# Routing stage of a two-layer MoE backbone rebuilt, and Hyena filter spectra summed on TensorE

## The chip, the cores and the metric

One NeuronCore of one Trainium2 chip runs the whole program. The metric is device time in microseconds of one execution, as a median of several runs. Engines are named as the profile names them: PE (TensorE), DVE (VectorE), ACT (ScalarE), POOL (GpSimd), SP (SyncE, which here only issues DMAs). All arithmetic is in float32.

## The reference, cut to what matters

The step runs two trunk layers on 128 context tokens and 256 latent tokens (384 together): an attention layer, a Hyena layer, and after each a hierarchical mixture of experts (top group of 4, then top 2 of the 8 experts in it; 32 experts of width 256).

```python
def hier_moe(h, ...):                       # once per layer
    g_w, g_i = top_k(softmax(t @ w_grp + b_grp), 1)
    e_logits = (t @ w_rt + b_rt).reshape(n, 4, 8)[arange(n), g_i[:, 0]]
    e_w, e_i = top_k(softmax(e_logits), 2)
    weights = e_w / sum(e_w) * g_w
    ...                                     # gates: one weight per token and expert
    hg, hu = t @ w_gate[e], t @ w_up[e]
    y = sum over e of (silu(hg) * hu * gates[:, e]) @ w_down[e]

def fft_longconv(u, kf, skip):              # twice in the Hyena layer, FFT length 2L
    y = irfft(rfft(u, 2 * L) * kf, 2 * L)[:L]
    return y + u * skip
```

`kf` is the spectrum of a filter made by a small network of the positions. The context group has L = 128 and the latent group L = 256.

## The kernel before

The engines run five separate programs and meet at semaphores; `sig(name).by` counts up after an instruction and `sig(name).at` waits. PSUM is eight banks of 128 x 512; `open_` takes the next bank (or a named one) and waits until its last reader has finished. A float32 matmul shows as several records.

**The MoE layer** (`moe(l)` on each engine, run for l = 0 and 1) has two parts. The *routing stage* starts when the last residual tile is normed. PE turns the normed tokens (`transposes`) and multiplies by the router (`logits`, three tiles of 128 tokens), then keeps itself busy with five dummy products (`keep_busy(5)`) while DVE picks group and experts. PE counts tokens per expert (`count`) and ranks them (`rank`, nine products, each of the three token tiles ending in one that waits for the count). DVE turns ranks into slots, and PE inverts that list (`pref`, `inv`): 768 slots in six tiles, ordered by expert. POOL then gathers the token rows of the six slot tiles out of DRAM by six indirect DMAs (L1842). PE sends four rows of tokens to all partitions (`rows`, from `diag`, twelve DVE products at L1288), then turns the six gathered tiles (L757, eight transposes a tile), and ACT and DVE evict half a tile each (`xs_a`, `xs_d`) into `XS`. After three more dummy products come the experts.

The *expert loop* goes through 32 experts in order, one *step* per 32 slots of an expert, and at least one. In a step POOL copies 32 slots of `XS` into `xcur` (L1859), PE multiplies by the gate and up weights (`hidden`), by the down weights of the step before (`down_product`), adds the step before's rows to the token sums (`first_half`, `second_half`) and regroups (`summed`), with ACT, DVE and POOL between. The first step has no step before; its sums are opened with zeros (`zeroed`). Weights stand in a ring of four expert slots of 3 MB. SP issues the loads of the first four experts as soon as the residual is done (`load_experts`), and each later one when ACT has freed its slot (`gu_free`, `down_free`).

**The Hyena layer** convolves two halves of 512 channels, twice (b = 0 to 3). For each b PE makes the filter's taps (`taps`, three products), their norms and six *spectra* K (`filter_spectra`): real and imaginary parts for the context group and for the even and odd positions of the latent group, of which two also get the skip term by a product of one row (`trow`). ACT copies four spectra out of PSUM, two of them into `KE`; DVE then adds and subtracts the other two (`combined`, four operations a b) to get the latent filter `KF`. PE makes the signal's spectra (`signal_spectra`, ten products), DVE multiplies (`product`), PE goes back (`inverse`), DVE gates (`gated`). The six signal spectra U and the six K share banks 0 to 5. While DVE multiplies for b, PE makes the spectra of b + 1, with four dummy products (`warm`) among them.

Of the kernel before, what the change touches and what calls it, by code (L numbers as in the profile page):

```python
# [25 lines left out]
P = 128  # L26
# [148 lines left out]
def build(nc, a, stage=99):  # L175
    ctx = ExitStack()
    with ctx:
# [245 lines left out]
        KE = v(WORK + 9232, 2, 512)  # L423
# [46 lines left out]
        def _(pe):  # L470
# [230 lines left out]
            def moe(l):  # L701
# [10 lines left out]
                logits(0)  # L712
                logits(1)
                transposes(u, (2,))
# [28 lines left out]
                for r in range(4):  # L743
                    i = l * 4 + r
                    o = open_(pe, "rows", i, [("posr" if r < 2 else "wr", l * 2 + r % 2)])
                    sig("diag").at(pe, i)
                    for t in range(T):
                        last = mm(o[:, t * P:(t + 1) * P], ones, diag[:, r, t, :])
                    close(last, "rows", i)
                for i in range(ST):  # L750
                    pe.wait_ge(rows_gathered[i], 16 * (l + 1))
                    for j in range(2):
                        n = (l * ST + i) * 2 + j
                        o = open_(pe, "xs", n, [("xs_a" if j == 0 else "xs_d", l * ST + i)])
                        for k in range(4):
                            c = (4 * j + k) * P
                            last = pe.transpose(o[:, k * P:(k + 1) * P], slot_rows[:, i, c:c + P], ident)  # L757
                        close(last, "xs", n)
                keep_busy(3)
                first = turn[0] + turn[0] % 2  # L760
                acc = [(("acc", l * 6 + i), [("xffn", l * 3 + (1 if i < 4 else 2))], (first + 2 + i) % 8) for i in range(6)]
# [94 lines left out]
            def hyena():  # L856
# [44 lines left out]
                def filter_spectra(b, j0, j1):  # L901
                    sig("filt").at(pe, b * 6 + 5)
                    for j in range(j0, j1):
# [4 lines left out]
                        if j >= 4:  # L908
                            sig("skip").at(pe, b * 2 + j - 4)
                            last = mm(o, ones[0:1, :], trow[j - 4][0:1, :], False, True)  # L910
# [1214 lines left out]
```

## Time and profile before

| | us |
|---|---|
| median of 3 runs (lowest, highest) | 1252.37 (1250.38, 1256.89) |
| the profiled execution | 1246.98 |
| its span, first to last instruction | 1245.2 |
| PE busy (share of the span) | 1131.2 (91%) |
| DVE busy | 563.9 (45%) |
| ACT busy | 266.5 (21%) |
| POOL busy | 176.0 (14%) |
| mean granted TensorE clock | 0.956 |

The profiled execution lies 5.4 us below the median. All times in rows are microseconds from the span's start. The granted clock is a share of 2.4 GHz: 1.00 is 2.4 GHz and 0.50 is 1.2 GHz, and a stretch between these was partly at either.

### The profile page before, as it was taken

The numbers are of one execution on the slowest core, as the hardware profiler recorded it, in microseconds if no ns is written. First come the engines' busy times: TensorE is split into PE (matmuls) and PEld (weight loads), VectorE is DVE, ScalarE is ACT, GpSimd is POOL, SyncE is SP. The second block draws the span as 40 slices with busy tenths as digits, with TensorE's granted clock in tenths as the row PEclk, the third lists the DMA queues.
The fourth block names the chain that finished last, engine by engine and source line by source line (L and its number), as shares of the span: only waits on it lengthen the run. The fifth ranks groups of instructions, "written<-read, shape, count | busy, mean of one in ns | idle before, by whom it ended". The sixth has DMA issues, their size and how long they took to land.

```text
span 1245.2 us, 26266 instructions
## 1 busy us (share of the span) xinstructions
PE 1131.2 (91%) x9219; PEld 647.4 (52%) x9220; DVE 563.9 (45%) x1222; ACT 266.5 (21%) x648; POOL 176.0 (14%) x261
## 2 busy tenths in 40 slices
PE   6899979989878899999699999999998888999995
PEld 4654656644654455555555654444546544555553
DVE  1031265544443344444633334787555344444445
ACT  2111244440121112212322113221011211221211
POOL 0153120000021111121100001111001111122220
PEclk9999999999788899999899998999996898999998
DMA  9856899740859899999831221000039599987893
GB/s 361 298 191 226 278 331 324 244 147 3 357 226 419 350 415 375 422 422 410 304 113 68 92 78 68 0 1 1 29 106 423 205 421 421 419 348 293 333 421 149
DMA packets 82735, 314.21 MB, mean 252 GB/s; under 512 B 11160, under 2 KB 12097, under 8 KB 57321
## 3 DMA queue, kind: packets, MB, share of 16 engines
q1 hardware_dynamic: 77658, 300.56, 62.1%
q0 software_dynamic: 1952, 6.90, 1.4%
q10 hardware_dynamic: 3056, 5.77, 1.2%
q8 instruction: 51, 0.84, 0.3%
q14 instruction: 18, 0.15, 0.0%
HBM read 307.82 MB, written 5.39 MB: 252 GB/s over the span
## 4 chain that ended last, share of the span: by engine, by line
PE 81%; DVE 5%; DMA 4%; issue 4%; ACT 2%; SPq 2%; POOL 1%; POOLq 0%; ACTq 0%; DVEq 0%
PE banks L472 78%; DMA arena<-in_ada_b 3%; DVE arena L1038 3%; DMA arena<-token_rows,arena 1%; PE banks L669 1%; SPq L1938 1%; PE banks L757 1%; ACT arena L1649 1%; SPq L1936 1%; ACT arena L1659 1%; DVE arena L1188 1%; POOL arena L1842 0%; PE banks L880 0%; PE banks L615 0%; PE banks L523 0%
## 5 line engine op out<-in xcount | busy, mean ns | idle before, releaser
L472 PE MATMUL banks<-arena 32*128 32x256 f32 (+10 forms) x8792 | 1076.0, 414 | 73.1 <-issue 34.2
L472 PEld LDWEIGHTS banks<-arena 128*32 128x32 f32 (+3 forms) x8792 | 595.0, 152 | 530.3 <-issue 402.0
L1038 DVE TENSOR_TENSOR arena<-banks,arena 128x64 f32<-128x64 f32 (+3 forms) x282 | 113.1, 413 | 65.6 <-PE banks L472 59.9
L1038 DVE TENSOR_TENSOR arena<-arena 128x384 f32<-128x384 f32 (+13 forms) x229 | 132.4, 584 | 4.4
L1307 DVE SCALAR_TENSOR_TENSOR arena<-arena 128x768 f32<-128x768 f32 x81 | 84.8, 1047 | 107.5 <-issue 105.2
L1693 ACT ACTIVATE arena<-banks 128x512 f32<-128x512 f32 x79 | 47.2, 597 | 230.6 <-PE banks L472 230.6
L1850 POOL TENSOR_TENSOR arena<-arena 128x256 f32<-128x256 f32 x81 | 59.1, 730 | 229.9 <-PE banks L472 229.9
L1317 DVE TENSOR_SCALAR arena<-arena 128x64 f32<-128x64 f32 x79 | 15.4, 195 | 163.9 <-ACT arena L1697 163.9
L1859 POOL COPY arena<-arena 128x256 f32 x79 | 34.7, 439 | 188.2 <-PE banks L472 148.6
L1829 POOL TENSOR_SCALAR arena<-arena 128x8 f32<-128x8 f32 (+2 forms) x28 | 6.8, 244 | 316.4 <-ACT arena L1540 229.0
L1407 DVE TENSOR_SCALAR arena<-arena 128x385 f32<-128x385 f32 x24 | 11.6, 481 | 82.4 <-ACT arena L1754 82.4
L1319 DVE RECIPROCAL arena<-arena 128x64 f32<-128x64 f32 x79 | 43.7, 554 | 2.7
L1697 ACT ACTIVATE arena<-banks 128x64 f32<-128x64 f32 x79 | 17.7, 224 | 127.3 <-PE banks L472 127.3
L1050 DVE COPY arena<-banks 128x128 f32<-128x128 f32 x24 | 7.0, 291 | 75.2 <-PE banks L472 75.2
L1689 ACT ACTIVATE arena<-banks 128x256 f32<-128x256 f32 x79 | 30.4, 384 | 42.4 <-PE banks L472 42.4
L1540 ACT ACTIVATE arena<-arena 128x1024 f32<-128x1024 f32 x12 | 12.7, 1056 | 113.1 <-DVE arena L1038 111.2
L1871 POOL TENSOR_TENSOR arena<-arena 128x512 f32<-128x512 f32 x4 | 5.1, 1263 | 208.9 <-DVE arena L1038 208.9
L1649 ACT ACTIVATE arena<-banks,arena 128x384 f32<-128x384 f32 (+1 forms) x48 | 24.0, 506 | 39.4 <-DVE arena L1189 31.4
L1830 POOL TENSOR_TENSOR arena<-arena 128x8 f32<-128x8 f32 (+2 forms) x28 | 30.5, 1091 | 2.4 <-POOL arena L1829 0.2
L1753 ACT ACTIVATE arena<-banks,arena 128x128 f32<-128x128 f32 x24 | 8.9, 369 | 100.3 <-PE banks L472 100.3
L1117 DVE TENSOR_REDUCE arena<-arena 128x8 f32<-128x512 f32 (+1 forms) x13 | 9.7, 745 | 43.3 <-ACT arena L1589 23.2
L669 PE MATMUL banks<-arena 128*128 128x128 f32 x112 | 16.8, 279 | 11.1 <-ACT arena L1659 11.0
(152 smaller groups left out, 456.6 us busy)
## 6 DMA issues: line engine op xcount, KB each, us to landing
arena<-in_moe_w_gate SPq DMA_DIRECT2D x64, 1024.0 KB, 8.0
arena<-in_moe_w_up SPq DMA_DIRECT2D x64, 1024.0 KB, 10.3
arena<-in_moe_w_down SPq DMA_DIRECT2D x64, 1024.0 KB, 10.6
arena<-in_ada_w SPq DMA_DIRECT2D x24, 2048.0 KB
arena<-in_hy_w_in SPq DMA_DIRECT2D x6, 2048.0 KB
arena<-in_attn_w_in SPq DMA_DIRECT2D x3, 2048.0 KB
arena<-mod_rows SPq DMA_DIRECT2D x8, 512.0 KB, 9.1
arena<-in_attn_w_out SPq DMA_DIRECT2D x2, 2048.0 KB
```

Source lines behind the costliest of these rows:

```text
L472: return pe.matmul(out, lhsT, rhs, start=start, stop=stop, skip_group_check=True)
L669: last = pe.transpose(o[:, b * P:(b + 1) * P], PB[i % 2][:, r, b, :], ident)
L1038: return dve.tensor_tensor(o, p, q, op)
L1307: return dve.scalar_tensor_tensor(parts, posr, first_row[:, bass.ds(c, 1)], wr, ALU.is_equal, ALU.mult)
L1319: dve.reciprocal(e2, e1).then_inc(s_["moe_dve"], 1)
L1649: ins = act.activation(PB[i % 2][:, r, 0:n, :].rearrange("p b k -> p (b k)"), ps[:, 2 * (i % 2) + r, 0:n * P], ACT.Exp, bias=negmax[:, c:c ...
L1689: act.activation(ysb, py, ACT.Copy).then_inc(s_["moe_y"], 1)
L1693: act.activation(gsb.rearrange("p i q f -> p (i q f)"), pg, ACT.Copy).then_inc(s_["moe_g"], 1)
L1697: act.activation(ex, pt[:, 0:2 * M].rearrange("p (f m) -> p f m", f=2), ACT.Exp, scale=-1.0).then_inc(s_["moe_e"], 1)
L1830: sig(name).by(pool.tensor_tensor(dst, dst, half_[:, 0:n], ALU.pow), i)
L1850: return pool.tensor_tensor(*two, bc(ones, 2), ALU.mult)
L1859: pool.tensor_copy(xcur, XS[:, :, bass.ds(first, M)]).then_inc(s_["moe_x"], 1)
```

## The change

Routing stage:

- The order of PE's first products is tiles 0, 1, logits 0, tile 2, logits 1, logits 2 (before: logits 1 ahead of tile 2).
- `rank` is four products in place of nine, one of them behind the count. `keep_busy(2)` behind it is gone.
- The two rows of gate weights are sent to all partitions ahead of `pref` and `inv`, the two rows of positions behind, as before. `diag` is four broadcast products of 128 x 384 in place of twelve of 128 x 128; two of them stand ahead of the slot arithmetic on DVE. `lanes` is one operation in place of six.
- The accumulators have fixed banks 2 to 7 and the six slot tiles are turned through the same banks. PE turns slot tiles 0 to 2, runs `hidden` of the first step, and then turns tiles 3 to 5. `keep_busy(3)` is gone.
- POOL reads the first expert's step count and copies its 32 slots as soon as slot tile 0 is evicted, ahead of its loop; the first expert's further steps, if any, and then experts 1 to 31 follow.
- SP issues the load of the fourth expert only when PE has turned slot tile 3.

Hyena stage: the combined spectra are summed in PSUM (cosine or sine of the even positions, plus or minus that of the odd ones), so `KE`, `combined` and the DVE operations in it are gone, and ACT copies six spectra per b. `warm` is gone. Three of the six spectra get the skip row.

```diff
                 transposes(u, (0, 1))
                 logits(0)
+                transposes(u, (2,))
                 logits(1)
-                transposes(u, (2,))
...
-                for t in (2, 1, 0):
-                    for s in range(t + 1):
-                        mm(o[:, t * NE:(t + 1) * NE], upper if s == t else ones, both[:, s, :], s == 0, False)
-                    sig("count").at(pe, l)
-                    last = mm(o[:, t * NE:(t + 1) * NE], cc[0:NE, 0:P], upE, False, True)
-                close(last, "rank", l)
-                keep_busy(2)
+                mm(o[:, 0:3 * NE], upper, both.rearrange("p t e -> p (t e)"), True, False)
+                mm(o[:, NE:3 * NE], ones, both[:, 0:2, :].rearrange("p t e -> p (t e)"), False, False)
+                mm(o[:, 2 * NE:3 * NE], ones, both[:, 0, :], False, False)
+                sig("count").at(pe, l)
+                close(mm(o[:, 0:3 * NE].rearrange("p (t e) -> p t e", t=T), cc[0:NE, 0:P], bc(upE, T, 1), False, True), "rank", l)
...
+                turn_rows(0)
+                turn_rows(1)
                 sig("steps").at(pe, l)
...
-                for i in range(ST):
-                    pe.wait_ge(rows_gathered[i], 16 * (l + 1))
-                    for j in range(2):
...
-                keep_busy(3)
+                turn_rows(2)
+                turn_rows(3)
...
+                turn_slots((0, 1, 2))
+                pe.wait_ge(gu_loaded[0], 32 + l * 32 * (NE // 4))
+                hidden(0, 0)
+                turn_slots((3, 4, 5))
...
-                        src, t, m = ((PM, 0, s128), (PM, 1, se), (PM, 2, so), (PF, 2, co), (PF, 0, c128), (PF, 1, ce))[j]
+                spectra = ((PM, ((s128, 0),), None), (PM, ((se, 1), (so, 2)), None), (PM, ((se, 1), (nso, 2)), None),
+                           (PF, ((ce, 1), (co, 2)), 1), (PF, ((ce, 1), (nco, 2)), 1), (PF, ((c128, 0),), 0))
...
-                filter_spectra(0, 2, 4)
+                filter_spectra(0, 2, 3)
                 taps(1, 0)
-                filter_spectra(0, 4, 6)
+                filter_spectra(0, 3, 6)
...
-                        warm(b, 4)
-                        filter_spectra(b + 1, 2, 4)
+                        filter_spectra(b + 1, 2, 3)
...
-                for c in range(6):
-                    ins = dve.tensor_scalar(lanes[:, c, :], lane, lane_of[:, c:c + 1], None, ALU.is_equal)
-                sig("lo").by(ins, l)
+                sig("lo").by(tt(lanes, bc(lane, 6, 1), bc(lane_of, P, 2), ALU.is_equal), l)
...
-                        tt(KF[:, 2 + im, :], e, o, ALU.add)
-                        sig("K_dve").by(tt(KF[:, 4 + im, :], e, o, ALU.subtract), b * 2 + j)
...
+                sig("pref").at(pool, l)
+                n, b = steps_of(pool, 0)
...
+                sig("xs_a").at(pool, l * ST)
+                sig("xs_d").at(pool, l * ST)
+                pool.wait_ge(s_["moe_pg"], 1)
+                pool.tensor_copy(xcur, XS[:, :, 0:M]).then_inc(s_["moe_x"], 1)
...
                 for s in range(4):
+                    if s == 3:
+                        sig("psum_xs").at(sp, (l * ST + 3) * 2 + 1)
                     one(s, s, None)
```

## Rows read from the trace of the kernel before

**Rows 1.** Page, chain that ended last: share of the span by engine.

```profile
PE 81%; DVE 5%; DMA 4%; issue 4%; ACT 2%; SPq 2%; POOL 1%; POOLq 0%; ACTq 0%; DVEq 0%
```

**Rows 2.** Windows: length, busy per engine (instructions), PEclk, DMA share, GB/s.

```profile
314.40:364.50 50.10, 39.58 (x192) 32.09 (x192) 23.73 (x79) 9.01 (x18) 7.89 (x13) 0.73 0.86 346
364.50:605.00 240.50, 221.23 (x2456) 118.74 (x2457) 103.51 (x229) 45.96 (x115) 43.18 (x76) 0.97 0.95 387
...
819.23:850.96 31.73, 31.73 (x77) 12.88 (x76) 25.25 (x37) 6.72 (x8) 3.99 (x4) 1.00 0.00 1
...
928.80:980.48 51.68, 42.19 (x198) 34.65 (x198) 23.71 (x79) 10.43 (x19) 7.93 (x13) 0.70 0.83 336
```

**Rows 3.** Timeline, first routing stage, end: start, duration, engine, line, [idle before <- releaser].

```profile
343.59 1.12 POOL L1842 DMA_INDIRECT arena<-token_rows,arena  x1 [23.70 <-DVE arena L1280]
...
350.04 0.93 POOL L1842 DMA_INDIRECT arena<-token_rows,arena  x1 [0.30 <-issue]
...
354.26 6.29 PE L757 MATMUL banks<-arena 128*128 128x128 f32 x40 [1.12 <-DMA arena<-token_rows,arena]
...
364.04 0.40 POOL L1859 COPY arena<-arena 128x256 f32 x1 [13.06 <-issue]
...
364.49 4.70 PE L472 MATMUL banks<-arena 128*32 128x512 f32 x48 [1.84 <-POOL arena L1859]
...
367.42 1.37 PEld L472 LDWEIGHTS banks<-arena 128*128 128x128 f32 x16 [0.33 <-ACT arena L1693]
```

**Rows 4.** Windows of 4 us around the gathers of the first routing stage.

```profile
340.00:344.00 4.00, 2.45 (x12) 2.35 (x12) 1.74 (x9) 0.00 (x0) 0.41 (x1) 0.50 1.01 422
...
356.00:360.00 4.00, 3.95 (x31) 3.71 (x30) 2.63 (x4) 1.81 (x4) 0.00 (x0) 0.84 0.37 149
...
368.00:372.00 4.00, 3.68 (x45) 1.72 (x44) 1.66 (x5) 0.72 (x2) 0.81 (x2) 1.00 0.22 45
```

**Rows 5.** DMA issues: median us from issue to landing, gathers (512 KB each) and outputs.

```profile
arena<-token_rows,arena POOLq DMA_INDIRECT x6, 9.2
...
out_y_sample<-arena ACTq DMA_DIRECT2D x2, 512.0 KB, 2.6
```

**Rows 6.** Timeline, DVE: slot arithmetic, and an operation of 128 x 384.

```profile
336.09 0.35 DVE L1038 TENSOR_TENSOR arena<-arena,banks 128x192 f32<-128x192 f32 x1 [1.37 <-PE banks L472]
...
338.02 1.26 DVE L1274 TENSOR_SCALAR arena<-arena 128x128 f32<-128x128 f32 x6
...
370.06 0.55 DVE L1038 TENSOR_TENSOR arena<-arena 128x384 f32<-128x384 f32 x1
```

**Rows 7.** Timeline, first routing stage, start: logits on PE, their reader on DVE.

```profile
316.40 4.01 PE L472 MATMUL banks<-arena 128*128 128x36 f32 x32 [2.01 <-ACT arena L1566]
...
322.94 8.92 PE L472 MATMUL banks<-arena 128*128 128x36 f32 x26 [0.78 <-ACT arena L1566]
...
326.57 0.27 DVE L1038 TENSOR_TENSOR arena<-banks,arena 128x108 f32<-128x108 f32 x1 [7.69 <-PE banks L472]
```

**Rows 8.** Windows, second routing stage: PE only turns slot tiles until 976.2.

```profile
971.60:975.00 3.40, 3.40 (x18) 3.40 (x17) 1.37 (x3) 1.19 (x2) 0.00 (x0) 0.50 0.11 45
975.00:978.40 3.40, 3.40 (x20) 2.31 (x18) 1.49 (x3) 1.20 (x2) 0.00 (x0) 0.99 0.02 5
```

**Rows 9.** Timeline, PE alone, Hyena's convolutions: where PE waited.

```profile
771.97 13.95 PE L472 MATMUL banks<-arena 128*128 128x512 f32 x26 [2.01 <-DVE arena L1038]
...
860.54 18.39 PE L472 MATMUL banks<-arena 128*128 128x512 f32 x76 [0.88 <-DVE arena L1038]
```

**Rows 10.** Windows in Hyena's convolutions where the clock was low.

```profile
770.40:777.20 6.80, 5.23 (x7) 2.21 (x8) 2.67 (x4) 1.68 (x2) 0.00 (x0) 0.51 0.01 2
800.90:804.40 3.50, 3.50 (x5) 1.52 (x5) 1.43 (x3) 2.08 (x2) 0.00 (x0) 0.51 0.00 0
```

**Rows 11.** Groups by shape, 761 to 900: count, busy us, mean ns, idle before.

```profile
L1038 DVE TENSOR_TENSOR arena<-arena,banks 128x512 f32<-128x512 f32 x16 | 10.2, 680 | 5.4 <-ACT arena L1776 5.4
...
L1776 ACT ACTIVATE arena<-banks 128x512 f32<-128x512 f32 x16 | 9.4, 597 | 60.2 <-PE banks L472 58.2 <-DVE arena L1409 1.9
```

More of the change, by code:

```diff
@@ L819, in four_experts @@
                     for s in range(4):
-                        pe.wait_ge(gu_loaded[s], (r + 1) * 32 + l * 32 * (NE // 4))
+                        if not (first and s == 0):
+                            pe.wait_ge(gu_loaded[s], (r + 1) * 32 + l * 32 * (NE // 4))
                         if first and s == 0:
-                            hidden(b, s)
                             for k, freed_by, bank in acc:
@@ L903, in filter_spectra @@
                     for j in range(j0, j1):
-                        src, t, m = ((PM, 0, s128), (PM, 1, se), (PM, 2, so), (PF, 2, co), (PF, 0, c128), (PF, 1, ce))[j]
+                        src, terms, skip = spectra[j]
                         i = b * 6 + j
-                        o = open_(pe, "K", i, [("K_dve", b * 2 + j - 2) if j in (2, 3) else ("K_act", b * 4 + (0, 1, None, None, 2, 3)[j])], j)
-                        last = mm(o, m, src[:, t, :], True, j < 4)
-                        if j >= 4:
-                            sig("skip").at(pe, b * 2 + j - 4)
-                            last = mm(o, ones[0:1, :], trow[j - 4][0:1, :], False, True)
+                        o = open_(pe, "K", i, [("K_act", i)], j)
+                        for q, (m, t) in enumerate(terms):
+                            last = mm(o, m, src[:, t, :], q == 0, skip is None and q == len(terms) - 1)
+                        if skip is not None:
+                            sig("skip").at(pe, b * 2 + skip)
+                            last = mm(o, ones[0:1, :], trow[skip][0:1, :], False, True)
                         close(last, "K", i)
-                def warm(b, n):
-                    o = open_(pe, "warm", b, [], 7)
-                    for _ in range(n):
-                        mm(o, ident, dft[:, 0:512])
                 def norm_columns(b):
@@ L1259, in moe @@
                 sig("steps").by(dve.tensor_scalar(cc[0:NE, P:2 * P], ci, 1.0, None, ALU.max), l)
+                for i in range(2):
+                    sig("diag").by(tt(diag[:, 2 + i], bc(ident, T, 1), bc(wt[i], P, 2), ALU.mult), l * 4 + i)
                 slot_of = read(dve, "rank", l)[:, 0:T * NE]
@@ L1476, in hyena @@
                 windowed(1, 0)
-                combined(0)
                 windowed(1, 1)
@@ L1482, in hyena @@
                         windowed(b + 2, 0)
-                    if b < 3:
-                        combined(b + 1)
                     gated(b)
@@ L1672, in moe @@
                 for r in range(2):
-                    sig("wr").by(act.activation(wr[:, r, :], read(act, "rows", l * 4 + 2 + r)[:, 0:NTOK], ACT.Copy), l * 2 + r)
+                    sig("wr").by(act.activation(wr[:, r, :], read(act, "rows", l * 4 + r)[:, 0:NTOK], ACT.Copy), l * 2 + r)
                 for i in range(ST):
```

87 lines of the change are left out of this document (44 added, 43 removed).

## Prediction

> **What bounds the kernel now.** I read the chain that ended last first: PE holds 81% of it, DMA 4%, DVE 5% [rows 1]. So PE's stretches decide, and an engine that gets less work gives nothing unless PE waits for it. Next the windows by stage [rows 2]. In Hyena's convolutions PE is busy for the whole 31.73 us of one b, while DVE is busy for 25.25: PE is the bound. In the expert loop PE is busy 221 of 240.5 us and the DMA queues 95% of it, at 387 GB/s: both are near their end, so an earlier start of the loop counts only if PE and the weight loads both start earlier. The two routing stages, 50.1 and 51.7 us, are different: PE is busy but at a mean clock of 0.73 and 0.70, and the DMA queues work 86 and 83% of the time.
>
> Then the timeline of the first routing stage's end [rows 3]. POOL issues six gathers from 343.6 to 351.0, one per 1.29 us ((350.04 - 343.59) / 5). PE turns the tiles until 360.5, waiting for "DMA arena<-token_rows", then dummies, then waits 1.84 us for POOL's copy, and the first `hidden` starts at 364.49. The gathers land 9.2 us after their issue (median), while 512 KB of output at the end of the kernel, with the queues empty, land in 2.6 [rows 5]. The reason stands in the DMA column: 422 GB/s at 340 to 344, and the queues dry up only between 356 and 360 [rows 4]. Between 316 and that point go four experts of 3.15 MB, 1.6 MB of stored tokens and 3.1 MB of gathered ones: 17.3 MB / 0.42 = 41 us, that is until 357. The gathers are last in a full queue.
>
> **Routing, the fourth expert held back.** Without it 9.4 + 1.6 = 11.0 MB are ahead of the gathers: 26 us, done at 342, before the first gather is issued. The landing then costs between 2.6 us (empty queue) and 9.2 (as now); I take 3.0, near the empty queue's row, because by this sum it is empty. The last tile, issued at 350.04, lands at 353.0 in place of 359.3. Held back, the fourth expert's load starts when slot tile 3 is turned (below, about 356), and its 3.15 MB take 7.5 us. The load for slot 0 queues behind it. In the trace before the queues are idle from 358 and start again only at 371.7 (45 GB/s as the mean of 368 to 372, [rows 4]); now the fourth expert fills them from about 357.3 to 364.8 and the next follows at once: the weight stream is 6.9 us earlier. The fourth expert is needed three steps after the first; steps of 5.5 us or more (the loop's first ones, bounded above by 240.5 / 32 = 7.5) put that at 370 or later, so it is not late itself. SP has nothing else behind that wait but the later experts.
>
> **Routing, the slot list itself.** Two edits pull against each other. `rank`: DVE waited 1.37 us for it [rows 6]; now one product follows the count, but two `diag` products of 128 x 384 (0.55 each, [rows 6]) fill the gap: -0.3. `lanes`: 1.26 us for six, against an estimated 0.95 for one of 768 columns, between once and twice 0.55: -0.3. PE has six products for the two weight rows ahead of `pref` and `inv`, in place of five of `rank` and two dummies: about even, -0.5 to +0.5. The new order of the logits: the 32 records of two tiles took 4.01 us, 2.0 a tile, but the last tile from 322.94 to 326.57 took 3.6, at 1.2 GHz [rows 7]. If the clock falls at the same time, two tiles run at 3.6 behind tile 2's turn, which costs 1.6 and saves the 0.78 us wait: about +0.8. If it stays up, the logits end some 2.5 earlier. Sum for the list: 0, with ends -2.5 and +1.5. I take 0: gathers issue at the same times as before.
>
> **Routing, from the gathers to the first step.** Turning a tile takes 1.7 us at 1.2 GHz (16 records; 18 in 3.4 us, [rows 8]), half of that at 2.4. Tiles 0 to 2 land at 346.6 to 349 and are turned by 351. POOL finishes its issue at 351.0 and reads two step numbers; before, the loop's entry with three took 2.7 us from the last eviction to the copy at 364.04. I take 1.3 plus the 0.40 copy: 352.7 (ends 351.9 and 354.1). `hidden` from 364.49 to the regrouping at 367.42 is 2.93 us with the zero product in it, of which I give 1.85 to `hidden`: until 354.6. Tiles 3 to 5 have landed: 2.8 us at 2.4 GHz, until 357.4. Then the last eviction (0.7), the zero product (1.1) and the gate copy in ACT's queue (0.7): regrouping at 359.9 against 367.42, 7.5 us earlier. POOL must now leave the first expert's block and enter the loop (2.7) after its move of the old rows, which can hold the second step by 0.5. So 7.0 us per stage on PE, and 6.9 on the weight stream: the whole loop moves by 7. The second stage has the same pattern; 14 us for both. Ends per stage: 3 (landing as now, clock low) and 9.5 (list 2.5 earlier).
>
> **Hyena.** A product of 512 columns costs 0.87 us: 31.73 less 0.46 of transposes over 36 products [rows 2]. Spectra were 8 products a b with the two skip rows, now 13 (1 + 2 + 2 + 3 + 3 + 2); three times four dummies go: 52 - 44 = 8 more, +7.0. DVE loses 16 operations, 10.2 us [rows 11], and this is worth only the waits of PE for them: 2.0 at 771.97, where the next taps need a bank that `combined` frees, and 0.88 at 860.54, where K and U share a bank that `product` frees [rows 9]; the first goes, of the second half stays: -2.5. ACT gets 8 copies of 0.6 more, hidden: it had 60 us idle for PE before these copies [rows 11]. Clock: PE ran at 1.2 GHz for 6.8 us from 770.4, through that wait, and for 3.5 from 800.9 [rows 10], just behind the spectra with one-row skip products. At half speed that lost 3.4 + 1.7 = 5.1 us. I expect the long one to shrink to a short one, as the wait goes, and the other to stay: -1.7. Sum +2.8, taken as +2.5. Ends: no fall at all -0.6; a short fall in each of the four passes +6.
>
> **Sum.** -14 + 2.5 = -11.5, rounded -12: 1246.98 goes to 1235 in a profiled execution. That execution lies 5.4 us below the median of the runs shown, so the median goes to 1252.37 - 12 = 1240.
>
> **Rivals.** (a) The gathers land as late as now, because POOL's path and not the full queue makes the 9.2 us. For it: every gather took 8.4 to 9.4, whatever its place. Against: the DMA column and the 17.3 MB. Then the last tile is in at 359.4, `hidden` is already done, and regrouping comes at 362.9: 4.5 a stage, -9 + 2.5 = -6.5: 1246.
> (b) PE turns tiles 3 to 5 and runs `hidden` and the first step at 1.2 GHz, since the dummies ahead of them are gone: +1.85 +2.5 +1.2 a stage, so 7 becomes 1.5: -3 + 2.5, no change: 1252. Against: in the second stage the clock was 0.50 from 971.6 and 0.99 from 975.0, with PE doing nothing but turn tiles between [rows 8]. The Trainium skill, TensorE: Matmul & The Clock Gate, Part 4, says that the full clock doesn't engage for transposes, as they don't count as PE-busy; by that rule (b) would be the forecast. The trace here does not agree: the clock rose during transposes alone, 0.50 to 0.99.
> (c) Slower: PE's clock. With the twelve `warm` products gone and three one-row products a pass in place of two, every pass drops to 1.2 GHz for as long as the one at 770.4 did: 4 x 3.4 - 5.1 = 8.5 lost against now, +7.0 - 2.5 = 4.5 of products: +13. With (b) in the routing stages, by the same cause, -3: +10, 1262. It decides once the falls in Hyena are about twice as long as now and the routing stages gain under 2 us each. Against: the pass from 819.23 held 1.00 throughout with the same skip rows [rows 2].
> (d) That the change does nothing: the list late by the logits and everything as in (a) gives 3 a stage, -6 + 6: 1252. I count it with (b).
>
> **How the numbers follow.** Forecast 0.68, (a) 0.15, (b) with (d) 0.11, (c) 0.06. Within the forecast the time runs from 1232 (9.5 a stage, -0.6) to 1248. The range 1230 to 1252 leaves out (c) and the edges. Half a per cent is 6.3 us, about what a measurement of this kernel can tell from no change. Faster by more: nearly all of the forecast and half of (a), 0.75; within: the rest of (a), (b) and a little of the forecast, 0.19; slower: 0.06.
>
> **What will show it.** Landing of the gathers near 3 us; DMA column near zero while they are issued, apart from them; the fourth expert's load a single block behind slot tile 3; first `hidden` between the turns at about 12 us ahead of its old place, the second step about 7; POOL's copy named as the releaser of the first `hidden`; no `combined` and no wait of 2 us at the first b; each b of Hyena 0.9 us longer. I am wrong if the gathers still need 9 us, if the loop starts earlier but then waits at the fourth or eighth expert for its weights, or if low-clock stretches appear in each pass of Hyena.

## The result and the profile after

The changed kernel takes 1248.1 us (median; 1242.4 to 1258.0) beside 1255.2 for the kernel before in the same measurement (1248.3 to 1259.9): ratio 0.9947, 95% interval 0.9926 to 0.9969. So it is 7.1 us faster by the medians (3.9 to 9.3 by the interval), where 12 were forecast. The profiled execution of after (1252.8 us, span 1251.1) is one of the longer ones, and 5 us of its span pass ahead of the change: its first routing stage starts at 319.18, that of before at 314.13. So single stretches are compared below and not spans.

The chain that ended last (page) has hardly moved, [rows 1]: PE keeps its 81%, "issue" has risen from 4 to 5%.

```profile
PE 81%; DVE 6%; issue 5%; DMA 4%; ACT 2%; SPq 2%; POOL 0%; ACTq 0%; POOLq 0%; DVEq 0%
```

Windows of after from the first weight load of a layer to the first sigmoid of its expert loop, and from there to the loop's last ACT operation of the same shape, a copy that closes the loop (columns as in [rows 2]):

```profile
319.18:365.87 46.69, 37.42 (x217) 30.87 (x215) 22.64 (x66) 9.86 (x19) 8.51 (x13) 0.74 0.86 334
365.87:597.22 231.35, 213.50 (x2404) 114.91 (x2408) 102.52 (x228) 45.06 (x114) 42.98 (x75) 0.98 0.99 407
...
930.88:976.11 45.23, 37.59 (x230) 30.92 (x230) 22.74 (x66) 11.15 (x20) 8.48 (x13) 0.77 0.89 344
976.11:1235.67 259.56, 234.21 (x2588) 124.08 (x2592) 110.84 (x246) 48.65 (x123) 45.71 (x81) 0.96 0.87 351
```

The same four stretches of before:

```profile
314.13:368.59 54.46, 43.93 (x237) 34.37 (x236) 23.73 (x79) 9.88 (x20) 8.92 (x14) 0.75 0.79 319
368.59:603.22 234.63, 215.86 (x2404) 115.98 (x2408) 101.94 (x227) 45.11 (x114) 42.15 (x74) 0.97 0.97 394
928.67:984.58 55.91, 46.30 (x242) 36.96 (x243) 23.71 (x79) 11.15 (x21) 8.97 (x14) 0.73 0.77 310
984.58:1229.65 245.07, 227.63 (x2588) 122.86 (x2592) 110.91 (x246) 48.72 (x122) 48.62 (x80) 0.98 0.89 364
```

The routing stages are 7.8 and 10.7 us shorter. The second loop, with the same 2588 records of PE, is 14.5 us longer. That is the surprise. The end of the first routing stage in after (timeline, to hold against [rows 3]):

```profile
348.05 1.12 POOL L1832 DMA_INDIRECT arena<-token_rows,arena  x1 [23.11 <-DVE arena L1286]
...
354.46 0.94 POOL L1832 DMA_INDIRECT arena<-token_rows,arena  x1 [0.31 <-issue]
...
355.95 0.39 POOL L1844 COPY arena<-arena 128x256 f32<-128x256 f32 x1 [0.56 <-issue]
...
357.95 1.93 PE L471 MATMUL banks<-arena 128*32 128x512 f32 x16
...
359.81 2.84 PE L763 MATMUL banks<-arena 128*128 128x128 f32 x24
...
360.93 0.33 SPq L2005 DMA_DIRECT2D arena<-in_moe_w_gate  x1
...
364.70 1.37 PEld L471 LDWEIGHTS banks<-arena 128*128 128x128 f32 x16 [0.33 <-ACT arena L1684]
```

The first `hidden` lies between the turns, the fourth expert's load goes out behind slot tile 3, and the regrouping comes 16.7 us after the first gather's issue, where it came 23.8 after it ([rows 3], 367.42 - 343.59). The gathers (DMA issues; windows of 2.5 and 4 us, against [rows 4, 5]):

```profile
arena<-token_rows,arena POOLq DMA_INDIRECT x6, 6.2
```

```profile
347.00:349.50 2.50, 0.64 (x3) 0.67 (x4) 2.38 (x8) 0.00 (x0) 1.15 (x2) 0.50 0.07 26
348.00:352.00 4.00, 2.90 (x12) 2.64 (x12) 2.51 (x7) 0.00 (x0) 3.04 (x4) 0.50 0.44 136
352.00:356.00 4.00, 2.88 (x13) 2.69 (x14) 1.49 (x3) 0.60 (x1) 2.83 (x4) 0.50 0.92 302
356.00:360.00 4.00, 3.62 (x30) 1.78 (x30) 1.38 (x2) 1.19 (x2) 0.35 (x1) 0.99 0.90 347
```

The queues do run dry ahead of them (0.07 between 347.0 and 349.5), and they land after 6.2 us in place of 9.2, not 3.0. The first gather, issued into these empty queues, already takes 5.0 us (4.6 in the second stage); once all are under way the queues are 90% busy with the gathers alone.

### The profile page after: what moved, and what is told of

Same layout as the page of the kernel before. It is cut to its first block, busy times and chain, and to the rows that moved or that the text cites. A ratio compares the mean times of both kernels' runs of the same rounds, so it can differ in the third digit from the quotient of the medians.

```text
span 1251.1 us, 26175 instructions
## 1 busy us (share of the span) xinstructions
PE 1129.4 (90%) x9195; PEld 642.1 (51%) x9196; DVE 550.7 (44%) x1180; ACT 271.4 (22%) x656; POOL 173.6 (14%) x261
## 4 chain that ended last, share of the span: by engine, by line
PE 81%; DVE 6%; issue 5%; DMA 4%; ACT 2%; SPq 2%; POOL 0%; ACTq 0%; POOLq 0%; DVEq 0%
PE banks L471 78%; DVE arena L1043 4%; DMA arena<-in_ada_b 3%; DMA arena<-token_rows,arena 1%; PE banks L668 1%; SPq L1944 1%; PE banks L763 1%; ACT arena L1640 1%; SPq L1942 1%; ACT arena L1650 1%; DVE arena L1193 1%; PE banks L887 0%; PE banks L614 0%; POOL arena L1832 0%; PE banks L522 0%
## 5 line engine op out<-in xcount | busy, mean ns | idle before, releaser
L471 PE MATMUL banks<-arena 32*128 32x256 f32 (+11 forms) x8768 | 1075.4, 416 | 81.5 <-issue 40.8
L471 PEld LDWEIGHTS banks<-arena 128*32 128x32 f32 (+4 forms) x8768 | 591.6, 153 | 540.1 <-issue 421.1
L1043 DVE TENSOR_TENSOR arena<-arena 128x384 f32<-128x384 f32 (+12 forms) x239 | 136.5, 579 | 4.5
L1684 ACT ACTIVATE arena<-banks 128x512 f32<-128x512 f32 x79 | 47.2, 597 | 228.3 <-PE banks L471 226.8
L1865 POOL COPY arena<-arena 128x256 f32 x77 | 31.1, 404 | 161.9 <-PE banks L471 158.3
L1766 ACT ACTIVATE arena<-banks 128x512 f32<-128x512 f32 x24 | 14.2, 597 | 58.9 <-PE banks L471 48.9
```

Of the source, the lines that this page charges most:

```text
L471: return pe.matmul(out, lhsT, rhs, start=start, stop=stop, skip_group_check=True)
L1043: return dve.tensor_tensor(o, p, q, op)
L1684: act.activation(gsb.rearrange("p i q f -> p (i q f)"), pg, ACT.Copy).then_inc(s_["moe_g"], 1)
L1865: pool.tensor_copy(xcur, XS[:, :, bass.ds(first, M)]).then_inc(s_["moe_x"], 1)
```

## Where the time went, over all traces

One trace is one execution, and the 16 runs below left 16 more, 18 in all. The lengths are differences of start times in the timelines: first weight issue by SP, first and last 128x64 activation of ACT in a loop, first product of 128x384 of Hyena. "Old" are the traces with the old form of the stage in question, "new" those with the new form and the fourth load behind slot tile 3. e13 and e14, which halve loads in the second loop, count in the stages ahead of it; e2, which resets the banks ahead of Hyena, is left out of the third row.

| stretch | old, mean (range), traces | new, mean (range), traces | difference | forecast |
|---|---|---|---|---|
| first routing stage | 54.5 (54.3 to 54.7), 4 | 46.7 (46.1 to 48.5), 6 | -7.8 | -7 |
| first loop | 237.0 (234.6 to 239.8), 4 | 231.9 (231.2 to 232.5), 6 | -5.1 | 0 |
| to Hyena's first product | 19.6 (18.8 to 20.6), 4 | 21.8 (21.3 to 22.6), 5 | +2.3 | 0 |
| Hyena layer | 309.3 (306.6 to 310.4), 5 | 310.4 (309.4 to 312.8), 13 | +1.1 | +2.5 |
| second routing stage | 54.8 (54.4 to 55.9), 4 | 45.9 (45.1 to 47.1), 6 | -8.9 | -7 |
| second loop | 244.4 (243.9 to 245.1), 3 | 257.0 (255.4 to 259.6), 5 | +12.6 | 0 |

The rows add up to -5.8, within the measured -3.9 to -9.3. The second loop has 41 steps in both kernels. The times from one step's sigmoid to the next (ACT's 128x64 activations) show that all of after's loss lies in the first eight intervals; from the ninth on before and after agree within 0.1 us (5.5 to 6.5 each), and within 0.2 in the short last one. In the repeats e1 and e16 the first eight hold 8.7 of 11.8 and 10.9 of 12.1 us:

| us between sigmoids | 1 | 2 | 3 | 4 | 5 | 6 | 7 | 8 | sum |
|---|---|---|---|---|---|---|---|---|---|
| before | 5.95 | 5.82 | 5.81 | 7.34 | 6.19 | 6.04 | 6.02 | 10.73 | 53.9 |
| after | 9.19 | 10.97 | 10.06 | 6.35 | 8.84 | 6.07 | 6.09 | 10.58 | 68.2 |
| e5, no hold-back | 5.71 | 5.72 | 5.61 | 7.62 | 6.93 | 6.06 | 6.02 | 9.23 | 52.9 |
| e6, late load | 7.13 | 5.62 | 6.40 | 7.71 | 7.21 | 6.31 | 6.05 | 7.91 | 54.3 |
| e9, late load and traffic | 8.10 | 10.48 | 8.17 | 9.34 | 6.17 | 6.05 | 6.02 | 9.71 | 64.0 |
| e10, late load, banks reset | 7.11 | 10.97 | 8.40 | 7.74 | 7.13 | 6.04 | 6.03 | 7.93 | 61.4 |
| e13, after, half the traffic | 7.14 | 6.73 | 7.61 | 9.13 | 6.17 | 6.06 | 6.03 | 6.66 | 55.5 |
| e14, before, half the traffic | 5.98 | 5.82 | 5.72 | 6.20 | 6.15 | 6.05 | 6.03 | 8.30 | 50.3 |

What PE does in the long intervals (timeline of after, PE alone; then the only two stops over 0.7 us in the first eight intervals of before):

```profile
977.03 2.35 PE L471 MATMUL banks<-arena 128*32 128x512 f32 x23 [0.31 <-issue]
982.29 3.62 PE L471 MATMUL banks<-arena 128*32 128x256 f32 x41 [2.91 <-issue]
986.11 1.92 PE L471 MATMUL banks<-arena 128*32 128x512 f32 x15 [0.20 <-issue]
991.02 6.97 PE L471 MATMUL banks<-arena 128*32 128x512 f32 x56 [3.00 <-issue]
1000.19 6.75 PE L471 MATMUL banks<-arena 128*32 128x512 f32 x57 [2.19 <-issue]
```

```profile
1004.54 5.57 PE L472 MATMUL banks<-arena 128*32 128x512 f32 x64 [1.77 <-issue]
...
1030.76 8.33 PE L472 MATMUL banks<-arena 128*32 128x512 f32 x64 [2.40 <-issue]
```

In the rows of after PE stops behind the 15th of the 16 records of `hidden`, or some records into the down product, for 2 to 3 us, and the releaser is "issue": no semaphore stands between two records of one product. It doesn't wait for weights: in all 18 traces PE's only other waits over 0.15 us in the second loop are one of 1.0 us for DVE and, in three of them, one of 0.3 us for POOL. Among the DMA packets there is one of an instruction queue, 16 KB, in or just ahead of each of these gaps (queues of after, 979.4 to 980):

```profile
q8 instruction: 1, 0.02, 10.6%
```

Such packets (blocks, below) started in after 3.7, 12.5 and 21.7 us behind the first sigmoid, and PE went on at 6.2, 14.9 and 24.1: 2.4 us behind each. In before they started at -7.1, 2.0, 10.1 and 15.6, and only one stall of 1.8 us, at 20, stands in the first 40. No view says whose instructions a packet holds; that they are PE's is concluded from this order in time, and it doesn't hold for every stall: of the 66 over 0.7 us in the first eight intervals of all traces, each by "issue", 34 end 2.3 to 2.7 us behind the start of such a packet and 32 end 3.2 to 6.0 us behind it. Over the first eight intervals the stalls over 0.7 us make 12.9 us in after and 4.2 in before. The clock takes the rest, as 991 to 995 shows:

```profile
987.00:991.00 4.00, 1.03 (x11) 0.12 (x3) 1.34 (x2) 0.00 (x0) 0.00 (x0) 1.00 0.94 309
991.00:995.00 4.00, 3.98 (x33) 1.89 (x33) 0.00 (x0) 0.98 (x2) 0.40 (x1) 0.58 0.90 346
```

The granted clock falls to the level of 1.2 GHz when PE goes on; behind the earlier stall of 2.91 us it did not fall. Summed over windows of 4 us, as 4 x (1 - clock), low clock costs 8.5 us in after and 3.4 in before: 8.7 by stalls and 5.1 by the clock are 13.8 of the 14.2. The same sum gives 7.8 of 8.7 us in e1 and 10.7 of 10.9 in e16.

The first loop's gain, which wasn't forecast, is in the main the same thing with the other sign. Its ninth interval takes 10.8 us in before and 6.3 in after (10.8 to 11.2 in three of the four old traces, 6.3 to 6.4 in the six new). PE's stops there, in before, then in after:

```profile
426.79 8.23 PE L472 MATMUL banks<-arena 128*32 128x512 f32 x64 [2.57 <-issue]
```

```profile
423.70 5.57 PE L471 MATMUL banks<-arena 128*32 128x512 f32 x64 [0.78 <-issue]
```

## The experiments

**Which part does it (e1 to e4).** e1 is the changed kernel again; e2 adds one line; e3 and e4 are the kernel before with only the routing part, or only the Hyena part, of the diff.

```diff
             if stage >= 3:
+                turn[0] += -turn[0] % 8          # e2
                 scaled_transposes(2)
```

> The changed kernel once more, for a second trace and more times. In its first trace the two routing stages were 7.8 and 10.7 us shorter, but the second expert loop, from its first regrouping to its end, took 263.0 us against 248.7, and gave all of that back. Theory A (chance): how PE's stalls in the first steps of a loop fall is different in each execution; the second loop comes out within 4 us of 248.7 here, and the span below that of the first trace. Theory B (the loop starts with three experts resident in place of four, and runs short of weights every time): the second loop is again 258 us or more.

> The changed kernel with one line more: behind the first MoE layer PE's bank counter is set on to a multiple of eight, so that the first transposes of the Hyena layer take banks 0 and 1, which are free when the experts end, and not banks 6 and 7, which the residual of the last token tile reads. Theory A: in the changed kernel the transposes waited 8.5 us for DVE against 5.7 before, and the stretch from the last expert product to the first Hyena product was 20.7 us against 17.1; with this line it is 17 again and the whole 3.5 us faster than the changed kernel. Rival: the transposes were waiting for the residual for another reason (the normalisation), and nothing changes.

> The kernel before with the routing stages of the change alone; the Hyena layer as before. Theory A: the Hyena part of the change costs 4.5 us, so this is 4.5 us faster than the changed kernel: about 11 us faster than before, ratio 0.991. Rival (the Hyena part is worth nothing or a gain, as its DVE work is gone): the same as the changed kernel or slower than it, 0.995 or more.

> The kernel before with the Hyena part of the change alone. Theory A: 4.5 us slower than before, ratio 1.0036, with the waits of 0.5 us for DVE and one skip product more in each b; no bank cost behind the first MoE layer. Rival: same as before within 1 us, or faster.

Ratios to before: e1 0.992 (0.9891 to 0.9949), e2 0.9926 (0.990 to 0.9952), e3 0.994 (0.9911 to 0.9969), e4 1.002 (0.9993 to 1.0048). The gain is the routing part's, and so is the loss in the second loop: 256.9, 255.4 and 255.8 us in e1 to e3, 243.9 in e4. So chance, e1's theory A, doesn't explain the loss, and theory B's reason, a shortage of weights, doesn't show in PE's waits. The Hyena part alone costs 2.1 us by the medians, not told from nothing; e3 and e4 both fall between their two expectations.

e2 shows the second place that the forecast lacked. In before the experts' banks follow the counter of banks; in the changed kernel they are fixed, and the counter stands at 6 and not at 0 when the turns ahead of Hyena open their banks. Banks 6 and 7 hold the sums of the last token tile. PE's wait there, in after, then in e2:

```profile
609.42 8.50 PE L471 MATMUL banks<-arena 128*128 128x128 f32 x48 [8.47 <-DVE arena L1043]
```

```profile
610.04 8.38 PE L471 MATMUL banks<-arena 128*128 128x128 f32 x48 [5.71 <-DVE arena L1083]
```

5.71 us is also what before waits at that point. The stretch to Hyena's first product is 19.7 us in e2 against 21.8 without the line. The whole time doesn't resolve it.

**Why the second loop loses (e5 to e9, e12).** Three theories were put against each other: T (traffic), R (ring) and L (layout), as the expectations say. e5, e6 and e8 change the order in the changed kernel, e7 adds traffic to the kernel before.

```diff
                 for s in range(4):
                     if s == 3:
-                        sig("psum_xs").at(sp, (l * ST + 3) * 2 + 1)    # e5: gone
+                        sp.wait_ge(gu_free[0], 1 + l * (NE // 4))      # e6
                     one(s, s, None)
+                sig("psum_xs").at(sp, (l + 1) * 2 * ST - 1)            # e7, in before
+                for i, w in enumerate((a["moe_w_gate"], a["moe_w_up"], a["moe_w_down"])):
+                    sp.dma_start(spare_d[l][i]..., w[l, 31]...).then_inc(spare_sem, 16)
...
                 turn_slots((0, 1, 2))
+                turn_slots((3, 4, 5))                                  # e8
                 pe.wait_ge(gu_loaded[0], 32 + l * 32 * (NE // 4))
                 hidden(0, 0)
-                turn_slots((3, 4, 5))                                  # e8
```

> The changed kernel, but SP issues the fourth expert's load together with the first three, as before the change. Measured so far in both kernels: the second expert loop, from its first sigmoid to its last, lasts 244 to 245 us with the old routing and 255 to 260 with the new one, all of it lost within the first 60 us. Theory T (traffic): PE's instruction blocks are fetched behind weight loads that now run from ahead of the loop's start; before, the queues were idle for the first 7 us of it. Theory R (ring): the loop starts with three experts resident in place of four and runs short of weights. Theory L (layout): the order of PE's code around the first hidden product makes it. Here the queues are idle at the loop's start again and four experts are resident: T and R both expect 244 to 247 us for the second loop, L 255 or more. All expect the gathers to land about 9 us after their issue, and the first regrouping some 3 us later than in the changed kernel. Whole time by T or R 1243, by L 1252.

> The changed kernel, but the fourth expert's load waits until the first expert's gate and up weights are done with (the point at which the next load for that slot is issued too). So the queues are empty while the gathers land and during the loop's first step, and the fourth expert comes about 8 us later than in the changed kernel. T (PE's instructions fetched behind weight traffic at the loop's start): the first stalls go, second loop 245 to 250 us. R (ring one expert short): worse than the changed kernel, PE waits for the fourth expert's weights, second loop 262 us or more. L (code layout): unchanged, 255 to 260. Gathers as in the changed kernel, 6 us.

> The kernel before with 3.15 MB of additional traffic: when the last slot tile is turned, SP copies one expert's weights from DRAM to a spare place in DRAM, which nobody reads. The queues are then busy during the first 7 us of both expert loops, in which they were idle; the first four experts are resident as before, and the weight loads of the fifth queue some 7 us behind. T: second loop 253 to 260 us in place of 244 to 245, with stalls of 1.5 to 3 us in mid product within the first 30 us. R: a weight stream 7 us later must show as waits for weights after the fourth expert, ahead of a product's first record. L: 244 to 247, no change.

> The changed kernel, but PE turns all six slot tiles and only then runs the first hidden product; the held-back load and all else stay. T and R: the second loop keeps its loss, 255 to 260 us. L: it goes back to 244 to 247. The first regrouping comes 0 to 2.5 us later than in the changed kernel (hidden's 1.85 us no longer lies in the wait for tiles 3 to 5).

| | ratio to before | routing stages | second loop |
|---|---|---|---|
| e5 | 0.9948 (0.9907 to 0.999) | 52.1, 51.5 | 243.6 |
| e6 | 0.9883 (0.9826 to 0.9941) | 46.1, 46.2 | 244.9 |
| e7 | 0.9986 (0.9959 to 1.0014) | 54.3, 54.5 | 244.2 |
| e8 | 0.9922 (0.989 to 0.9955) | 46.8, 45.9 | 253.2 |

R falls, since PE waits for weights in none of these traces. L falls with e8, which undoes the early first product and keeps most of the loss; e5 and e6 keep that product and lose nothing, but each is one trace, and the same kernel as e6 did lose when it ran again (e15, below). T holds in e5 and e6 and fails in e7. e5 pays for its loop elsewhere: its routing stages are 5 to 6 us longer than the changed kernel's, and it is 5.8 us faster than before by the medians, where 12 were expected. e7's windows say why T may have missed there: the copy ran from 8 us ahead of the first sigmoid to 1.5 behind it, while PE waited for other things, and the queues were quiet (70 GB/s) when the next block came at 3.0. So e9 puts the same traffic where the changed kernel has it, on top of e6, and e12 puts a third of it there.

```diff
                     if s == 3:
                         sig("psum_xs").at(sp, (l * ST + 3) * 2 + 1)
+                        # e9: the three copies of e7 here;  e12: the gate weights' load here
+                        sp.wait_ge(gu_free[0], 1 + l * (NE // 4))
```

> As the kernel with the late fourth load (issued when the first expert's gate and up weights are done with), but with a copy of 3.15 MB of weights from DRAM to a spare place in DRAM, which nobody reads, issued when slot tile 3 is turned: the same bytes at the same moment as the changed kernel's fourth load. All waits of PE, the ring and the order of the code are those of the late kernel; only the traffic from 5 us ahead of the first sigmoid to 3 us behind it differs. Theory T (a block of PE's instructions that is fetched in that stretch comes late, and PE runs one block behind from there): the second loop loses again, 253 to 260 us in place of 244.9, with stalls of 2 to 3 us in mid product at about 4 to 15 us. Theory P (what counts is the time at which the weight stream starts against PE's steps, not the traffic): 244 to 247, as in the late kernel, or at most the 5 us later landing of the first weights, shown as waits for weights.

> The changed kernel, but of the fourth expert only the gate weights (1.05 MB, 2.5 us) are issued when slot tile 3 is turned; up and down weights wait as in the late kernel. T: the queues are quiet again 2.5 us ahead of the first sigmoid, and the block of instructions that the late kernel fetched at -1.5 comes then: second loop 244 to 248. P: half-way, the stream starts at the early time: 250 to 256.

The theories are now T and P (what counts is when the weight stream starts against PE's steps). e9 took 1.0013 of before (0.9983 to 1.0042) beside 0.9883 for e6, which ran on another chip, and its second loop 254.7 us, as T expected; e12 0.9915 (0.9882 to 0.9947) and 250.6, in the range of P, with 3 us of its loss behind the eighth interval. Windows ahead of the loop and PE's waits in it, e6:

```profile
976.00:980.00 4.00, 3.02 (x35) 2.48 (x32) 2.35 (x4) 1.79 (x3) 0.73 (x1) 1.00 0.02 4
980.00:984.00 4.00, 4.00 (x27) 1.60 (x30) 2.45 (x6) 0.22 (x1) 1.12 (x2) 0.61 0.22 57
```

```profile
979.74 15.48 PE L471 MATMUL banks<-arena 128*128 128x32 f32 x150
995.41 5.12 PE L471 MATMUL banks<-arena 128*32 128x512 f32 x57 [0.18 <-issue]
1002.67 5.57 PE L471 MATMUL banks<-arena 128*32 128x512 f32 x64 [2.14 <-issue]
```

and e9, with the same waits in its code:

```profile
976.00:980.00 4.00, 3.02 (x34) 2.48 (x32) 2.35 (x4) 1.68 (x3) 0.73 (x1) 1.00 1.01 360
980.00:984.00 4.00, 4.00 (x27) 1.40 (x31) 2.13 (x6) 0.22 (x1) 1.12 (x2) 0.57 1.19 414
```

```profile
993.69 7.01 PE L473 MATMUL banks<-arena 128*32 128x512 f32 x56 [2.45 <-issue]
1002.63 5.12 PE L473 MATMUL banks<-arena 128*32 128x512 f32 x57 [1.93 <-issue]
```

In e6 PE's first stop over 0.7 us comes 21.9 us behind the first sigmoid; in e9 there is one at 13.3 and one at 22.2. That speaks against P, if the two traces stand for their kernels; the next runs say that e6's doesn't.

**Does the late load repair it (e10, e11, e15, e16).** e10 is e6 with the line of e2; e11 is the same with the old Hyena stage; e15 and e16 are e6 and the changed kernel again.

> The changed kernel with the late fourth load and with the rotation of PSUM banks set back to bank 0 ahead of the turns that lead into the Hyena layer. T: second loop 243 to 247 us; P: the same, since the late kernel has shown 244.9. From the last step of the first loop to the first Hyena product 19 to 20 us in place of 22.5. By the segments 255 less 7.3, 8.5 and 1.5 plus 4: about 1241.5.

> As the run before this one, with the Hyena stage of before (combined spectra on DVE, warm products). By the segments the spectra on PE cost 1.8 to 3.7 us, so 1238 to 1240 in place of 1241.5; if the waits that DVE causes are worth more than the added products, it is slower by up to 1.

> The kernel with the late fourth load once more. If it is a repair (T in its simple form), the second loop lasts 244 to 248 us again and the median lies 4 us or more below that of the changed kernel on this chip. If the first trace fell on a good execution, 250 to 255 and a median within 2 us of the changed kernel's.

> The changed kernel once more, to stand beside the run before this one on the same chip: second loop 255 to 260 us as in its two traces so far if the loss belongs to its order of loads; anything below 250 would say that the loss is a matter of the single execution.

Ratios: e10 0.9921 (0.9893 to 0.9949), e11 0.9918 (0.9888 to 0.9949), e15 0.9916 (0.9878 to 0.9954), e16 0.9951 (0.9927 to 0.9975). Second loops: 252.1, 254.2, 253.2 and 257.2 us. So the late load takes off a part (251.1 as the mean of e6, e10, e11 and e15 against 257.0), not the whole, and what e6 showed, the three later traces did not. e10 misses what both theories expected (243 to 247), and e11, with the old Hyena stage, is not the 2 to 4 us faster than e10 that it was to be. In e10 the blocks came at 1.2, 10.4 and 19.6 us without any added traffic, the first of them ahead of the first weight issue (at 1.3), and PE waits as in e9:

```profile
991.71 6.93 PE L471 MATMUL banks<-arena 128*32 128x512 f32 x56 [3.00 <-issue]
```

By the trace of the second loop e10 (252.1) takes back most of what e9 (254.7) seemed to show. The medians don't: e9 and e10 ran on the same chip, and their ratios, 1.0013 and 0.9921, have intervals that don't meet, so the same bytes at the entry do cost some 1%. Whether they cost it by late instructions, or by the time that they take in the queues ahead of the weights, isn't told apart; e10 also has the line of e2, which by e1 and e2 makes no difference that the times resolve. No version beats the changed kernel by more than the intervals.

**Is it the traffic at all (e13, e14).** Both ran once, for the trace. Both halve the loads of the second loop from the fifth expert on; only half of each of these experts' weights is replaced, so the second layer's experts are computed with mixed weights.

```diff
                         src = w[l, bass.ds(e, 1)].rearrange("o (p k) n -> p (o k) n", k=KC)
+                        if l == 1 and uses is not None:
+                            dst, src = dst[:, 0:KC // 2], src[:, 0:KC // 2]
...
+                    if l == 1 and uses is not None:
+                        down, src = down[:, 0:1], src[:, 0:1]
```

> The changed kernel, but in the second expert loop the loads from the fifth expert on bring only half of each expert's gate, up and down weights (the output's second layer is not the reference's; instructions, waits and steps of PE are the same, and the routing of the second layer too). So the queues are some 50 to 60% busy there in place of 95%. Theory T (instruction blocks are late because they are fetched behind weights): after the fourth expert's load, which is still whole, the stalls of 2 to 3 us in mid product go, at most the first (about 4 to 6 us into the loop) stays; second loop 238 to 244 us. Rival U (PE cannot fetch faster, whatever the queues carry; the new entry into the loop has only cost it its lead): stalls at the same places as in the changed kernel, second loop 253 to 260.

> The kernel before with the same halved loads in the second expert loop. T: its stalls at 20 us (1.8) and, if it is one of these, at 46 us (2.4) go: 240 to 244 us in place of 245. U: both stay, 244 to 246. A stall that stays here and in the run before this one at the same step has another cause, in the steps themselves.

The loops take 249.9 and 240.5 us. The first 60 us of the loop in after (976.11) and in e13:

```profile
976.11:1036.11 60.00, 46.06 (x456) 22.90 (x456) 20.71 (x47) 8.65 (x22) 8.98 (x16) 0.91 0.95 372
```

```profile
976.46:1036.46 60.00, 53.07 (x564) 26.79 (x568) 24.30 (x54) 10.83 (x27) 11.99 (x19) 0.94 0.71 242
```

With 35% less traffic PE gets 108 records more done in the same time. The stalls over 0.7 us fall from 12.9 to 4.3 us, in before from 4.2 to 1.1 (its stall at 20 us goes, the one ahead of the eighth interval shrinks from 2.4 to 1.1). Both first sums lie below those of every trace with whole loads and the same entry (55.5 against 62.6 to 68.2 in five, 50.3 against 53.6 to 54.0 in three), so the load of the queues has a part in the stalls, as far as one trace each can show. It isn't all of e13's gain. Its first block came 1.25 us behind the first sigmoid, ahead of the first halved load (issued at 1.5), where those five have 2.2 to 4.1; at entries of 1.0 to 1.2 us e8, e10 and e15, with whole loads, took 60.2 to 61.4. So by these traces the halving is worth some 5 us, as an estimate, and the earlier block the rest. Neither theory has 249.9: it lies between T's 238 to 244 and U's 253 to 260. Over the first eight intervals e13 still needs 5.3 us more than e14, and two intervals far behind these take 8.2 in place of 6.4, as in e1.

What stays open is why the blocks come when they do. e6 and e15 are the same kernel, with no weights under way at the entry in either; the block came 1.0 us ahead of the first sigmoid in e6 and 1.0 behind it in e15, and the first eight intervals took 54.3 and 60.2. Nor does that time alone decide: in e11 it came as early as in e6, and they took 63.3. The first loop stalls in both kernels and doesn't suffer from the new entry (before 8.61, 8.17, 8.47 and 10.81 among its first nine intervals, after 8.99, 7.06, 9.86 and 7.32), although the block comes there 3.8 to 4.3 us behind the first sigmoid in the new form. Moving PE's code against the blocks was not tried.

## Why the prediction was right or wrong

**Gathers: right in kind, wrong in size.** "I take 3.0, near the empty queue's row": 6.2. The queue ahead is empty as the sum of bytes said, but the row was that of another kind of transfer, and alone: the first gather, with nothing ahead of it, takes 5.0 us, and six of 0.5 MB, issued every 1.28 us, are a queue of their own. The landing's end at 9.2 had been kept in the range.

**The stage: right, a little better, with two misses that nearly cancel.** 7 us per stage forecast, 7.8 and 8.9 measured. `hidden` started at 357.95, 9.9 us after the first gather's issue (forecast 352.7 - 343.6 = 9.1). POOL's copy didn't release it, as I had put it, but was done 1.6 us earlier; PE came from turning tile 2, which by the later landing ended 10.0 us after that issue and not 7.4 (351 - 343.6). A turned tile is 8 records, not 16; the 1.7 us at 1.2 GHz held all the same (two tiles in 3.43). The list gained 0.6 us in the first stage and 2.2 in the second (first weight issue to first gather, 27.6 us against 29.8), where 0 was taken.

**"The whole loop moves by 7": the step that failed.** It holds to the first sigmoid only. Weights and PE both start earlier, as the argument asked, but the loop's own length was taken as unchanged, and it isn't: PE's stalls by "issue" in the first eight intervals of the second loop grow from 4.2 to 12.9 us, and the low clock costs 5.1 us more. The gain of the second stage (8.9) and more (12.6) was lost again, in after's own trace within 68 us. That these stalls are instruction blocks that come late is concluded from the packets' times, that the load of the queues has a part in it from e13 and e14; why the new entry meets them worse is open. The first loop, also forecast at 0, gave 5.1 us, in the main in one interval with a shorter stop, and that the time still fell to 1248, inside the stated 1230 to 1252, is that much luck. The prediction also bounded the loop's first steps by 7.5 us, from 240.5 / 32; that loop has 38 steps, with up to 10.8 us among its first nine. "I am wrong if the loop starts earlier but then waits at the fourth or eighth expert for its weights" was looked for in the wrong place: PE never waited for weights there. The trace of before could have raised the doubt, since stalls of 1.8 and 2.4 us by "issue" stand in its second loop.

The Trainium skill, Runtime: NRT & Kernel Launch, Instruction fetch mechanics, says that the sequencer fetches the next block of 256 instructions over a DMA queue of its own while it executes the present one, and that this is mostly hidden. The packets of 16 KB agree with the block; "mostly hidden" doesn't hold in the first eight intervals here, if the stalls are these fetches: 12.9 us of them in after, 4.3 in e13 with half the loads.

**Rotation of banks: not seen.** +2.3 us, though the change names the fixed banks. What a counter leaves for the next stage belongs to the price of a fixed bank.

**Hyena: +1.1 for +2.5 forecast, within its ends, by other terms.** A pass is 1.84 longer, not 0.87 (33.57 against 31.73 us): the added skip product takes about 1.2 (two records of 640 ns), and `product` frees a bank 0.54 us late for each b:

```profile
790.09 28.88 PE L471 MATMUL banks<-arena 128*128 128x512 f32 x64 [0.54 <-DVE arena L1043]
...
823.65 6.87 PE L471 MATMUL banks<-arena 128*128 128x512 f32 x15 [0.54 <-DVE arena L1043]
```

The wait of 2.0 us at the first b is gone, as forecast. The clock gave back more than forecast: of the 6.8 and 3.4 us at 1.2 GHz in [rows 10] after has one stretch of 3.4 left, the short one, which was to stay, being gone too. Over all traces the old form has 10.2 to 17.1 us at 1.2 GHz in the convolutions (mean 15.0), the new 0 to 6.8 (mean 2.1); at half speed that is some 6 us, as an estimate, where 1.7 was forecast. before's own trace had been a short one (306.6 us, the other old ones 309.1 to 310.4).

**Rivals.** (a), gathers as late as before, did not come true: 6.2 us. Nor did (b), low clock in the turns and the first step: the clock is 0.50 until 356 and 0.99 from there, 2 us ahead of the first `hidden` and with turns alone on PE since 353.1. The rule of the Trainium skill, TensorE: Matmul & The Clock Gate, Part 4, that transposes don't bring the full clock, isn't borne out in this trace either. (c) and (d), slower and no change, did not come true. A further one, that the loop itself gets longer because PE stops for its instructions, was missing.

## What to carry to other kernels

An earlier start of a stream of loads is worth what PE makes of it in the steps behind it: compare the step times one by one, not the start of the loop. A stall by "issue" in the middle of a product points to instructions, and halving the traffic with all waits kept tests whether the queues have a part in it. One trace of a kernel is not its rule: e6 lost nothing and e15, the same kernel, 8.8 us (253.2 against 244.4). Where a hand-written bank replaces a counter, follow the counter to its next user.

## What the runs showed of the hardware

- Of 66 stalls of PE over 0.7 us (first eight intervals of the second loop, 18 traces), all by "issue", 34 ended 2.3 to 2.7 us behind the start of a 16 KB instruction packet, the others 3.2 to 6.0. With the queues 95 to 98% busy (first 60 us of the loop) they lasted up to 3.3 us, with some 70% (e13 and e14) up to 1.9.
- Some of these stalls come with a fall of the granted clock to the 1.2 GHz level, which costs another 1.7 us (4 x 0.42 in the row at 991): four of the six in after, two of the six in e1.
- Six gathers of 0.5 MB in a row move 302 to 347 GB/s (352 to 360 in after), while weights in the same kernel reach 420 GB/s. The first of them, issued into empty queues, landed after 5.0 us (4.6 in the second stage).
